# The in-projection's common stage with its pieces moved on every engine, and the recurrence's receptance copied on chip

## The chip, the cores and the metric

The kernel runs on one core of one Trainium2 chip, as a single launch. The metric is the device time of one execution in microseconds; of the kernel before, three runs were timed (2557.12, 2568.69 and 2574.31 us, median 2568.69 us). The engines are called as in the profile: PE is TensorE (PEld its weight loads), DVE is VectorE, ACT is ScalarE, POOL is GpSimd and SP is SyncE, which here only starts DMAs.

## What is computed

Two layers of a flow-matching backbone on 1024 latent and 256 context tokens of width 1024. The even layer has one projection to queries, keys, values, streams of an RWKV-7 mixer and gates; a dense attention and a two-way recurrence read these; an output projection closes the layer. The odd layer has windowed attention in their place. The change lies in the even layer, between its projection and its recurrence. What is computed there, cut from the reference:

```python
p = p + mu * (0.5 * (pp[:, :-2] + pp[:, 2:]) - p)
r, k, v, zw, za = jnp.split(p, ...)
w_log = -jax.nn.softplus(-(w0 + jnp.einsum('btdr,drc->dbtc', jnp.tanh(zw), w2))) - 0.5
decay = jnp.exp(-jnp.exp(w_log))
a = jax.nn.sigmoid(a0 + jnp.einsum('btdr,drc->dbtc', za, a2))
kkf = heads(k * k_k)
kk = kkf / jnp.maximum(jnp.sqrt(jnp.sum(kkf * kkf, axis=-1, keepdims=True)), 1e-12)
kmod = k * (1 + (a - 1) * k_a)
# recurrence, per direction d, head and token, with b = kk * a
S = S * w_t - (S kk_t) b_t + v_t k_t ;   y_t = S r_t
bonus = sum(r * kmod * rk) * v
```

The kernel runs the recurrence in chunks of 64 tokens, so the stage before it has to leave in memory, for each direction, four streams (receptance, removal key, b and key), each multiplied by the exponential of a running sum of decay rates, up or down.

## The kernel before

**Stages.** The program is a sequence of stages on one core: `in0`, the projection of layer 0 (`projected`, from 0 to 672 us of the span), `chunked_scan` (to 1254), dense attention (to 1584), an output projection (to 1765), the projection of layer 1 (to 2095), window attention (to 2446) and the last output projection.

**The order of `in0`.** A hand-written list `order` holds ten steps that turn tokens, then 84 units. A unit is one job's weight block (128 output columns) over one segment of tokens: 28 jobs by three segments, 512, 512 and 256 tokens. It takes 24 matmuls (three split products by eight blocks of the inner dimension, `split_products`, L164). Each engine has its own loop over `order` and its own in-order program; semaphores tie them. At unit i PE computes product i, ACT reads unit i-1 out (at the units of gates with a silu), and DVE finishes unit i-1: for a gate one multiplication of 0.68 us per 512 tokens (L857), at a job's end the split of the weights of the job after next into two parts (L847, L849), and for a mix job the blend with the neighbours (L864, L867). POOL adds the neighbours of a mix job (L700) and issues the stores.

**Jobs.** `jobs0` is: two gates (units 0 to 5), key (6 to 8), value (9 to 11), four queries (12 to 23), fourteen mix jobs (24 to 65), six gates (66 to 83). The first two mix jobs are the low-rank inputs z of the rates; the twelve others are key, receptance and value of four pairs of heads.

**The common stage.** Between the units each engine runs pieces of what makes the streams: `items` has 60 pieces, four pairs of heads by (5 N + 10 X), each on 256 tokens. An N piece normalises a block of keys: a square on ACT, a sum over the head on PE (`squares`, L1132), a clamp on DVE (L938), reciprocal root and square on ACT (L592, L594), and three DVE operations (`unit_keys`, L944 to L950). An X piece makes the streams of one direction: two small matmuls on PE (`loras`, L1142 and L1143), two tanh and a scaling on ACT (`rates`), a scan and a subtraction on DVE (`sums`, L961 and L963), three exponentials on ACT (`exponentials`, L617 to L620), seven DVE multiplications (`products`, L976 to L993), at every second piece two more (`bonus_of`) and the turning of the values on PE and ACT (`turn_values`, L1150, `values_out`, L635), and the stores on POOL.

`slot_of_unit` says which pieces run at which unit, and each engine's `slot(t)` which part of which piece. Before, pieces start at unit 40, the first five at one per unit and then 1.35 per unit; on PE a unit's pieces stand behind its product, and each engine takes the parts of piece t or t-1. SP loads the inputs of the pieces from unit 37 on (`load_z` L437, with `CLEAR_AT` 36: POOL clears buffers that alias those of earlier units first), then keys and receptances as they become ready.

**The recurrence.** `chunked_scan` walks 20 groups in software-pipelined periods. A group has a tile `L` of streams (two directions, two pairs) and a tile `RI`, in which an identity and the receptance lie side by side; `RI` has two buffers. Its identity part is loaded once per buffer (16 DMAs, L1298), its receptance part by eight DMAs per group from the streams in memory (`load_reads`, L1272), though the same values are in `L` already. DVE adds it to a product at `EQ`, which waits for the loads (`r_in`).

## Time and profile before

| | us |
|---|---|
| median of three runs | 2568.69 (2557.12 to 2574.31) |
| profiled execution | 2581.38 |
| its span | 2579.6 |
| PE busy | 2130.2 (83%) |
| DVE busy | 1292.5 (50%) |
| ACT busy | 871.7 (34%) |
| POOL busy | 722.2 (28%) |
| mean granted clock of PE | 0.916 |

The span is the time from the first to the last instruction that the profiler recorded; the execution's own time is 1.8 us more. The profiled execution lies 12.7 us (0.5%) above the median. The busy share of PE is an average over stages with different limits, so the rows further down are of single stages: the units with pieces (313 to 627 us), the end of `in0`, and the recurrence. The clock is a share of full speed (1.0 is 2.4 GHz, 0.5 is 1.2 GHz).

### The profile page before, as it was taken

Reading aid. Unit: us, or ns where it says so; the run is one execution under the profiler, and the core shown is the slowest. Engines: PE = TensorE matmul, PEld = TensorE weight load, DVE = VectorE, ACT = ScalarE, POOL = GpSimd, SP = SyncE. Lnnn points to the kernel's source line nnn. Section 1 sums busy time; section 2 is a strip of 40 time slices with the busy share of each in tenths; the row PEclk is TensorE's granted clock in tenths of the full one; section 3 lists DMA queues with packets and bytes.
Section 4 is the critical chain, followed back from the end, with each engine's and each line's share of the span. In section 5 each row is a group of like instructions: output and inputs, shape, how many; then the busy total and the mean of one; then the engine's idle time right before and its main releaser. Section 6 shows DMA issues by size and latency. Waiting matters only on the chain. (4 is left out here: it accounts for less than half of the span.)

```text
span 2579.6 us, 61157 instructions
## 1 busy us (share of the span) xinstructions
PE 2130.2 (83%) x26174; PEld 1790.7 (69%) x26174; DVE 1292.5 (50%) x2064; ACT 871.7 (34%) x1685; POOL 722.2 (28%) x786
## 2 busy tenths in 40 slices
PE   3899998787367888878599996894999969999988
PEld 1667876565257777777488885673777758888866
DVE  4335467886334444444354443985546524444422
ACT  2223144465234434444133332222334302333311
POOL 2246322211123224233041000343357414100012
PEclk6999998898589999999799997896999979999989
DMA  8556444553322222220321104644344453111162
GB/s 296 180 145 161 131 143 152 180 182 127 112 80 80 64 81 70 61 86 24 87 82 42 42 27 138 189 140 162 105 110 110 112 140 99 58 50 51 39 201 90
DMA packets 228941, 285.70 MB, mean 111 GB/s; under 512 B 61529, under 2 KB 166905, under 8 KB 227649
## 3 DMA queue, kind: packets, MB, share of 16 engines
q1 hardware_dynamic: 190624, 176.52, 22.9%
q0 software_dynamic: 25680, 81.58, 9.9%
q10 hardware_dynamic: 12368, 23.70, 3.1%
q8 instruction: 209, 3.42, 0.6%
q14 instruction: 60, 0.48, 0.1%
HBM read 193.76 MB, written 87.95 MB: 109 GB/s over the span
## 5 line engine op out<-in xcount | busy, mean ns | idle before, releaser
L164 PE MATMUL in_acc<-in_hi,in_whi 128*128 128x512 f32 (+1 forms) x1024 | 400.6, 391 | 19.6 <-DVE in_lo L840 17.6
L164 PE MATMUL in_acc<-in_lo,in_whi 128*128 128x512 f32 (+1 forms) x1024 | 379.6, 371 | 0.0
L164 PE MATMUL in_acc<-in_hi,in_wlo 128*128 128x512 f32 (+1 forms) x1024 | 379.4, 371 | 0.0
L164 PEld LDWEIGHTS in_acc<-in_hi,in_whi 128*128 128x128 f32 x1024 | 199.2, 195 | 72.3 <-issue 42.3
L164 PEld LDWEIGHTS in_acc<-in_lo,in_whi 128*128 128x128 f32 x1024 | 199.2, 195 | 35.2 <-issue 5.3
L164 PEld LDWEIGHTS in_acc<-in_hi,in_wlo 128*128 128x128 f32 x1024 | 198.5, 194 | 33.2
L1939 DVE TENSOR_REDUCE window_top<-window_score 128x1 f32<-128x640 f32 (+1 forms) x128 | 101.3, 791 | 185.2 <-PE window_score L2022 185.1
L1939 DVE TENSOR_REDUCE dense_top<-dense_score 128x1 f32<-128x640 f32 (+1 forms) x144 | 112.3, 780 | 162.0 <-PE dense_score L2026 161.8
L2064 PEld LDWEIGHTS dense_outs<-dense_V,dense_p 128*128 128x128 f32 x1344 | 169.5, 191 | 8.5 <-ACT dense_p L1907 4.9
L2064 PE MATMUL dense_outs<-dense_V,dense_p 128*128 128x65 f32 x1344 | 169.9, 269 | 0.9 <-ACT dense_p L1907 0.8
L2064 PE MATMUL window_outs<-window_V,window_p 128*128 128x65 f32 x1216 | 160.8, 276 | 1.6 <-ACT window_p L1907 1.1
L2064 PEld LDWEIGHTS window_outs<-window_V,window_p 128*128 128x128 f32 x1216 | 153.2, 195 | 9.1 <-ACT window_p L1907 2.6
L1460 DVE TENSOR_TENSOR scan_X<-scan_X,scan_small 128x512 f32<-128x512 f32 x80 | 55.0, 688 | 188.3 <-PE scan_small L1588 187.1
L1593 PE MATMUL scan_wide<-scan_XT,scan_Y 64*64 64x64 f32 x3200 | 120.8, 223 | 24.9 <-issue 24.7
L2238 POOL MEMSET close_eps<- 128x1 f32 x2 | 0.2, 103 | 474.5 <-POOLq L127 474.5
L1338 POOL TENSOR_TENSOR scan_DG<-scan_LB,scan_lmask 128x512 f32<-128x512 f32 x20 | 25.3, 1266 | 382.9 <-ACT scan_LB L1374 382.9
L1907 ACT ACTIVATE dense_p<-dense_turned 128x512 f32<-128x512 f32 x168 | 96.1, 597 | 107.7 <-PE dense_turned L2050 107.2
L164 PE MATMUL close_acc<-w_hi,close_hi 128*128 128x512 f32 x288 | 117.3, 407 | 18.2 <-DVE close_lo L2312 18.2
L1569 PE MATMUL scan_small<-scan_X,scan_off 64*64 64x64 f32 x3200 | 119.9, 226 | 11.2 <-issue 10.4
L1593 PEld LDWEIGHTS scan_wide<-scan_XT,scan_Y 64*64 64x64 f32 x3200 | 106.7, 135 | 25.0 <-issue 24.9
L1347 POOL TENSOR_TENSOR scan_off<-scan_LA,scan_lmask 128x512 f32<-128x512 f32 x100 | 124.0, 1274 | 0.0
L1388 ACT ACTIVATE scan_Y<-scan_small 128x512 f32<-128x512 f32 x100 | 59.7, 597 | 189.8 <-PE scan_small L1569 189.8
(268 smaller groups left out, 5161.6 us busy)
## 6 DMA issues: line engine op xcount, KB each, us to landing
streams<-in_streams_out POOLq DMA_DIRECT2D x40, 512.0 KB, 3.8
scan_L<-streams SPq DMA_DIRECT2D x80, 256.0 KB, 3.7
in_wl<-in_w_mod ACTq DMA_DIRECT2D x32, 512.0 KB, 4.5
in_raw<-in_w_in_even SPq DMA_DIRECT2D x28, 512.0 KB, 4.3
in_raw<-in_w_in_odd SPq DMA_DIRECT2D x20, 512.0 KB, 4.0
close_ga<-gates SPq DMA_DIRECT2D x18, 512.0 KB, 4.1
in_wm<-in_w_mod SPq DMA_DIRECT2D x8, 1024.0 KB, 12.3
gates<-in_outs POOLq DMA_DIRECT2D x32, 256.0 KB, 3.7
```

The lines of the kernel that those rows point to most:

```text
L164: last = pe.matmul(out, a(k), b(k), start=(k == 0 and x == 0), stop=(k == n - 1 and x == 2))
L1338: pool.tensor_tensor(DG[:], LB[:], lmask[:, 0:1, :].to_broadcast([P, NU, HD]), ALU.mult).then_inc(diagonal, 1)
L1347: pool.tensor_tensor(off[s][:, k], triangles, lmask[:, k + 1:k + 2, :].to_broadcast([P, NU, HD]), ALU.mult).then_inc(off_done, 1)
L1388: act.activation(Y[s][:], small[s][:], ACT.Copy).then_inc(y_read[s], 1)
L1460: dve.tensor_tensor(X[s][:], X[s][:], small[s][:], ALU.subtract).then_inc(x_less[s], 1)
L1569: return pe.matmul(small[s][half_of(1 - c), u, :], off[s][half_of(c), k, u, :], X[s][half_of(c), u, :], start=True, stop=True)
L1593: return pe.matmul(wide[s][half_of(1 - c), u, :], Y[s][half_of(1 - c), u, :], XT[j % 3][half_of(1 - c), u, :], start=True, stop=True)
L1907: act.activation(p[:, s % NP_], turned[s % NTURN][:], ACT.Exp, scale=SCALE).then_inc(expd, 1)
L1939: dve.tensor_reduce(top[:, i % NSLOT, x, r:r + 1], score[:, :, 0:width], AXS, ALU.max).then_inc(topped, 1)
L2064: last = pe.matmul(outs[i % 2][:, r * HW:(r + 1) * HW], p[:, s % NP_, r * P:(r + 1) * P], v, start=(k == 0 and r == 0), stop=(k == n - 1 a ...
L2238: pool.memset(eps[:, 0:1], EPS).then_inc(readied, 1)
```

## The change

It does the following.

1. **Pieces.** They start at unit 38 and are spread evenly, 63 slots (60 pieces and three to flush) over 50 units. A slot t issues parts of different pieces: on PE the first low-rank product of piece t+2, the second of t+1, the squares of t+1 and the turned values of t-1, and all of it stands ahead of the unit's product; on ACT the exponentials of t-1, rates of t+1, roots of t-1, squares of t+2, values out of t-2; on DVE first the last part (unit keys, products, bonus) of t-2 and then clamp or sums of t; on POOL the stores of t-3.
2. **One exponential less.** A tile `falls` holds the falling exponential with one extra column of ones per chunk, so that the receptance reads it at one offset and the removal key at the other; DVE's subtraction and ACT's second exponential are gone, and a POOL memset is added. DVE's scaling of `km` moves to ACT. `sigs` and `km` get more buffers. The squares go to a PSUM bank of their own (`aux` 3), the second low-rank product has one bank in place of two.
3. **Loads of z.** Two DMAs in place of four.
4. **Jobs.** Five mix jobs come first (units 0 to 14), then key, value, queries (15 to 32), nine mix jobs (33 to 59) and all eight gates (60 to 83).
5. **Recurrence.** `load_reads` is gone; ACT copies the receptance from `L` into `RI` (four copies of 64x256 per group). `RI` has three buffers, so 24 identity loads in place of 16, and SP's load of the streams of group a+2 waits for the copies of group a too.

```diff
-    CLEAR_AT, N_AT = 36, 40
+    CLEAR_AT, N_AT, FLUSH = 36, 38, 3
-        slot_of_unit[u] = min(len(items) + 1, max(0, min(u - N_AT, NSG) + max(0, (u - N_AT - NSG) * 27 // 20)))
+        slot_of_unit[u] = max(0, u - N_AT) * (len(items) + FLUSH) // (NU + 4 - N_AT)
...
 # SP, load_z
-                    sp.wait_ge(cleared, 3)
+                    sp.wait_ge(cleared, 4)
                     sp.dma_start(tz[:], rkvz[12]).then_inc(z_in, 16)
-                    for d in range(2):
-                        sp.dma_start(za[(1 - d) * HD:(2 - d) * HD], rkvz[13][d * HD:(d + 1) * HD]).then_inc(z_in, 16)
-                        sp.dma_start(a2s[(1 - d) * HD:(2 - d) * HD], a2[d]).then_inc(dc_in, 16)
+                    sp.dma_start(za[:], rkvz[13]).then_inc(z_in, 16)
+                    sp.dma_start(a2s[:], a2.rearrange("d r n -> (d r) n")).then_inc(dc_in, 16)
...
 # ACT, rates(b, s, d)
+                    act.wait_ge(sig_done, n + 1)
+                    if q >= 2:
+                        act.wait_ge(bon_sum, q - 1)
+                    act.activation(km[:, q % 2, d], sigs[:, n % 3], ACT.Identity, scale=kac[:, b:b + 1], bias=kan[:, b:b + 1]).then_inc(mixed_k, 1)
 # ACT, exponentials(b, s, d)
-                    act.activation(e_to[:], cum[:, h], ACT.Exp, scale=-DECAY).then_inc(exp_to, 1)
-                    act.activation(before[:, h], before[:, h], ACT.Exp, scale=-DECAY).then_inc(exp_in, 1)
+                    act.activation(falls[:, d, :, 1 - d:CHUNK + 1 - d], cum[:, h].rearrange("p (c n) -> p c n", n=CHUNK), ACT.Exp,
+                                   scale=-DECAY).then_inc(exp_to, 1)
 # ACT, slot(t)
                     if item(t - 1)[0] == "X":
                         exponentials(*item(t - 1)[1:])
...
+                    if item(t + 1)[0] == "X":
+                        rates(*item(t + 1)[1:])
+                    if item(t - 1)[0] == "N":
+                        root_keys(*item(t - 1)[1:])
+                    if item(t + 2)[0] == "N":
+                        square_keys(*item(t + 2)[1:])
+                    if item(t - 2)[0] == "X" and item(t - 2)[3] == 1:
+                        values_out(*item(t - 2)[1:3])
...
 # DVE, slot(t)
+                    if item(t - 2)[0] == "N":
+                        unit_keys(*item(t - 2)[1:])
+                    if item(t - 2)[0] == "X":
+                        products(*item(t - 2)[1:])
+                        if item(t - 2)[3] == 1:
+                            bonus_of(*item(t - 2)[1:3])
                     if item(t)[0] == "N":
                         clamp(*item(t)[1:])
                     if item(t)[0] == "X":
                         sums(*item(t)[1:])
-                    if item(t - 1)[0] == "N":
-                        unit_keys(*item(t - 1)[1:])
-                    if item(t - 1)[0] == "X":
-                        products(*item(t - 1)[1:])
-                        if item(t - 1)[3] == 1:
-                            bonus_of(*item(t - 1)[1:3])
...
 # PE
                 def squares(b, s):
                     q = q_of(b, s)
-                    side_free()
+                    if q >= 1:
+                        pe.wait_ge(clamped, q)
                     pe.wait_ge(squared_k, q + 1)
-                    pe.matmul(side[:, 0:SG], block1[:], ksq[:, q % 2], start=True, stop=True).then_inc(squares_in, 1)
+                    pe.matmul(aux[:, 3, 0:SG], block1[:], ksq[:, q % 2], start=True, stop=True).then_inc(squares_in, 1)
+                def lora_of_a(b, s, d):
+                    n, half = n_of(b, s, d), slice(d * HD, (d + 1) * HD)
+                    if n >= 1:
+                        pe.wait_ge(sig_done, n)
+                    pe.matmul(aux[:, 2, 0:SG], a2s[half, b * P:(b + 1) * P], za[half, s * SG:(s + 1) * SG], start=True, stop=True
+                              ).then_inc(lora_a, 1)
                 def slot(t):
                     if t == 0:
                         pe.wait_ge(tanhed, 1)
-                    if item(t)[0] == "N":
-                        squares(*item(t)[1:])
-                    if item(t)[0] == "X":
-                        loras(*item(t)[1:])
-                        if item(t)[3] == 1:
-                            turn_values(*item(t)[1:3])
+                        squares(0, 0)
+                    if item(t + 2)[0] == "X":
+                        lora_of_w(*item(t + 2)[1:])
+                    if item(t + 1)[0] == "X":
+                        lora_of_a(*item(t + 1)[1:])
+                    if item(t + 1)[0] == "N":
+                        squares(*item(t + 1)[1:])
+                    if item(t - 1)[0] == "X" and item(t - 1)[3] == 1:
+                        turn_values(*item(t - 1)[1:3])
...
                     else:
+                        for t in slots(what, i):
+                            slot(t)
                         if i < NU:
                             product(i)
...
-                    for t in slots(what, i):
-                        slot(t)
...
 # recurrence
-        RI = [st.sb(f"RI{s}", [P, NU, P]) for s in range(2)]
+        RI = [st.sb(f"RI{s}", [P, NU, P]) for s in range(3)]
...
                         sp.wait_ge(gram_in, 2 * a + 2)
+                        sp.wait_ge(reads_done, a + 1)
                         load_streams(a + 2)
...
-                    if c is not None and c + 2 < NG:
-                        sp.wait_ge(eq_read, 2 * c + 2)
-                        load_reads(c + 2)
...
+                def reads(j):
+                    s = j % 2
+                    act.wait_ge(l_in[s], uses(j) * 4 * 16)
+                    if j >= 3:
+                        act.wait_ge(eq_read, 2 * (j - 3) + 2)
+                    for c in range(2):
+                        for h in range(2):
+                            last = act.activation(RI[j % 3][half_of(c), 4 * h:4 * h + 4, half_of(c)].rearrange("p (d g) n -> p d g n", g=2),
+                                                  L[s][half_of(h), :, :, half_of(c)], ACT.Copy)
+                    last.then_inc(reads_done, 1)
...
                     if a is not None:
                         turned_out(a, 2)
+                        reads(a)
...
-    jobs0 = (gates[:2] + key_jobs(QC, AKV, kst0) + value_jobs(QC + AKV * HD, AKV, v0) + query_jobs(0, AH, qst0, 3) + mixes
-             + gates[2:])
+    jobs0 = (mixes[:5] + key_jobs(QC, AKV, kst0) + value_jobs(QC + AKV * HD, AKV, v0) + query_jobs(0, AH, qst0, 3) + mixes[5:]
+             + gate_jobs(GA, gates0, 3))
```

How the order of instructions moves is shown at two places.

**VectorE, in a gate's unit with a weight split, where the last X piece of a pair of heads meets the first N pieces of the next.** `in_whi` and `in_wlo` are the two parts of the split weights, `in_norm` the clamped sum of squares, `in_outs` the gated output of the unit. Before:

```order
L857 SCALAR_TENSOR_TENSOR in_outs<-in_xs,in_acc 128x256 [waits in0_out_stored2,in0_sig]
L847 CAST in_whi<-in_raw 128x1024 [waits in0_summed,in0_w_in0]
L849 TENSOR_TENSOR in_wlo<-in_raw,in_whi 128x1024 [waits in0_w_high]
L938 TENSOR_SCALAR in_norm<-in_side 128x256 [waits in0_unit,in0_squares_in]
L976 SCALAR_TENSOR_TENSOR in_b_<-in_sigs,in_kk 128x256 [waits in0_b_done,in0_kd_done,in0_unit,in0_sig_done]
L979 TENSOR_SCALAR in_km<-in_sigs,in_kac,in_kan 128x256
L982 TENSOR_TENSOR in_km<-in_km,in_rkv 128x256 [waits in0_rkv_in0,in0_mixed_k]
L986 TENSOR_TENSOR in_streams_out<-in_rkv,in_e_to 128x2x128 [waits in0_exp_to,in0_s_stored1]
L988 TENSOR_TENSOR in_streams_out<-in_kk,in_before 128x2x128 [waits in0_exp_in]
L991 SCALAR_TENSOR_TENSOR in_streams_out<-in_b_,in_cum 128x2x128 [waits in0_b_made,in0_exp_from]
L993 TENSOR_TENSOR in_streams_out<-in_km,in_cum 128x2x128 [waits in0_km_done]
L999 TENSOR_TENSOR in_bon<-in_km 128x256 [waits in0_bon_stored]
```

With the change, at the same place of the pieces (the end of a pair's X pieces):

```order
L863 SCALAR_TENSOR_TENSOR in_outs<-in_xs,in_acc 128x256 [waits in0_out_stored2,in0_sig]
L853 CAST in_whi<-in_raw 128x1024 [waits in0_summed,in0_w_in0]
L855 TENSOR_TENSOR in_wlo<-in_raw,in_whi 128x1024 [waits in0_w_high]
L987 SCALAR_TENSOR_TENSOR in_b_<-in_sigs,in_kk 128x256 [waits in0_b_done,in0_unit,in0_sig_done]
L990 TENSOR_TENSOR in_km<-in_km,in_rkv 128x256 [waits in0_rkv_in1,in0_mixed_k]
L994 TENSOR_TENSOR in_streams_out<-in_rkv,in_falls 128x2x128 [waits in0_exp_to,in0_s_stored1]
L995 TENSOR_TENSOR in_streams_out<-in_kk,in_falls 128x2x128
L998 SCALAR_TENSOR_TENSOR in_streams_out<-in_b_,in_cum 128x2x128 [waits in0_b_made,in0_exp_from]
L1000 TENSOR_TENSOR in_streams_out<-in_km,in_cum 128x2x128 [waits in0_km_done]
L1006 TENSOR_TENSOR in_bon<-in_km 128x256 [waits in0_bon_stored]
L1008 SCALAR_TENSOR_TENSOR in_bon<-in_rkv,in_rkc,in_bon 128x256 [waits in0_bon_sum]
L944 TENSOR_SCALAR in_norm<-in_aux 128x256 [waits in0_unit,in0_squares_in]
```

The clamp (`in_norm`, from `in_aux` now and from `in_side` before) stands behind the last part of the X piece, where it stood ahead of it; the subtraction and the scaling of `km` are no longer in the row of operations.

**TensorE, at a unit that takes two X pieces.** `in_aux` takes the low-rank products, `in_side` the turned values, `in_acc` the unit's product. Before:

```order
L1142 MATMUL in_aux<-in_tz,in_w2s 128x256 [waits in0_sig_done,in0_rate_t]
L1143 MATMUL in_aux<-in_za,in_a2s 128x256
L1142 MATMUL in_aux<-in_tz,in_w2s 128x256 [waits in0_sig_done,in0_rate_t]
L1143 MATMUL in_aux<-in_za,in_a2s 128x256
L1150 MATMUL in_side<-in_ident,in_rkv 128x128 [waits in0_rkv_in1,in0_values_read,in0_clamped]
L1150 MATMUL in_side<-in_ident,in_rkv 128x128
L164 MATMUL in_acc<-in_hi,in_whi 128x256 [waits in0_gated,in0_low,in0_w_low]
```

With the change:

```order
L164 MATMUL in_acc<-in_hi,in_wlo 128x512
L1140 MATMUL in_aux<-in_tz,in_w2s 128x256 [waits in0_rate_t]
L1147 MATMUL in_aux<-in_za,in_a2s 128x256 [waits in0_sig_done]
L1156 MATMUL in_side<-in_ident,in_rkv 128x128 [waits in0_rkv_in0,in0_values_read]
L1156 MATMUL in_side<-in_ident,in_rkv 128x128
L1140 MATMUL in_aux<-in_tz,in_w2s 128x256 [waits in0_rate_t]
L1147 MATMUL in_aux<-in_za,in_a2s 128x256 [waits in0_sig_done]
L164 MATMUL in_acc<-in_hi,in_whi 128x256 [waits in0_gated,in0_low,in0_w_low]
```

The last row of each is the first matmul of a 256 wide product: before that of the next unit, now that of the pieces' own unit. Before, the six matmuls stood behind their unit's product; now they stand ahead of their own unit's product, and each second low-rank product (L1147) waits for ACT to have read the one before (`in0_sig_done`), where before two banks took turns.

## Rows read from the trace of the kernel before

**Rows 1.** Windows: us; PE, PEld, DVE, ACT, POOL busy (count); clock; DMA share; GB/s.
```profile
313.00:627.00 314.00, 268.75 (x1329) 213.61 (x1329) 239.11 (x485) 156.39 (x381) 73.94 (x94) 0.91 0.49 157
627.00:672.00 45.00, 4.97 (x20) 2.06 (x18) 25.86 (x67) 14.93 (x44) 7.50 (x14) 0.56 0.40 135
760.00:1254.00 494.00, 394.43 (x15475) 369.68 (x15467) 230.99 (x383) 202.04 (x374) 148.44 (x120) 0.97 0.22 63
```

**Rows 2.** Waits of TensorE from 313 to 627 us: total us, times, longest us.
```profile
PE in_side L1132 <- issue: 20.4, 3, 9.3
PE in_side L1150 <- ACT in_vt_out L635: 13.7, 4, 4.6
```

**Rows 3.** Timeline of TensorE: first matmuls of three products (512, 256 and 512 wide).
```profile
308.00 0.39 PE L164 MATMUL in_acc<-in_hi,in_whi 128*128 128x512 f32 x1
...
313.44 0.28 PE L164 MATMUL in_acc<-in_hi,in_whi 128*128 128x256 f32 x1
...
316.31 0.40 PE L164 MATMUL in_acc<-in_hi,in_whi 128*128 128x512 f32 x1
```

**Rows 4.** Timeline of VectorE over one X piece: start us, us, what, [idle before, releaser].
```profile
619.23 0.69 DVE L961 TENSOR_TENSOR_SCAN in_cum<-in_carry,in_rate 128x256 f32<-128x256 f32 x1
619.95 0.42 DVE L963 TENSOR_TENSOR in_before<-in_cum,in_rate 128x256 f32<-128x256 f32 x1
...
622.75 0.68 DVE L857 SCALAR_TENSOR_TENSOR in_outs<-in_xs,in_acc 128x512 f32<-128x512 f32 x1
624.86 0.69 DVE L961 TENSOR_TENSOR_SCAN in_cum<-in_carry,in_rate 128x256 f32<-128x256 f32 x1 [1.42 <-ACT in_rate L604]
```

**Rows 5.** Timeline of ScalarE: an X piece from its first exponential, and a table load.
```profile
562.34 0.42 ACT L617 ACTIVATE in_e_to<-in_cum 128x256 f32<-128x256 f32 x1 [2.58 <-issue]
...
565.51 0.58 ACT L523 ACTIVATE in_xs<-in_acc 128x512 f32<-128x512 f32 x1
...
590.96 1.28 ACT L523 ACT_TABLE_LOAD   x1
592.25 0.60 ACT L523 ACTIVATE in_xs<-in_acc 128x512 f32<-128x512 f32 x1
```

**Rows 6.** Timeline around the start of the pieces: VectorE, SyncE's queue twice, TensorE.
```profile
303.53 3.23 DVE L849 TENSOR_TENSOR in_wlo<-in_raw,in_whi 128x1024 fp32r<-128x1024 f32 x1
...
307.28 0.50 SPq L439 DMA_DIRECT2D in_tz<-rkvz  x1
...
319.45 0.50 SPq L455 DMA_DIRECT2D in_k_all<-rkvz  x1
...
327.22 0.59 PE L1132 MATMUL in_side<-in_ksq,in_block 128*128 128x256 f32 x2
```

**Rows 7.** Timeline of VectorE over an N piece behind a weight split.
```profile
599.54 0.69 DVE L847 CAST in_whi<-in_raw 128x1024 fp32r<-128x1024 f32 x1
...
601.40 0.42 DVE L938 TENSOR_SCALAR in_norm<-in_side 128x256 f32<-128x256 f32 x1
...
602.65 0.48 DVE L950 SCALAR_TENSOR_TENSOR in_kk<-in_k_all,in_kkn,in_norm 128x256 f32<-128x256 f32 x1
```

**Rows 8.** Timeline: VectorE's last operation of the first stage.
```profile
657.61 0.48 DVE L1001 SCALAR_TENSOR_TENSOR in_bon<-in_rkv,in_rkc,in_bon 128x256 f32<-128x256 f32 x1
```

**Rows 9.** Timeline at the start of the recurrence: SyncE's queue three times, TensorE.
```profile
680.19 10.40 SPq L1298 DMA_DIRECT2D scan_RI<-in_consts  x16
690.64 5.57 SPq L1272 DMA_DIRECT2D scan_RI<-streams  x8
...
720.10 5.15 SPq L1272 DMA_DIRECT2D scan_RI<-streams  x8
...
731.77 1.97 PE L1531 MATMUL scan_gram<-scan_ident,scan_L 128*128 128x128 f32 x8 [18.79 <-DMA scan_L<-streams]
```

**Rows 10.** Timeline of ScalarE in the middle of the recurrence.
```profile
980.06 0.77 ACT L1402 ACTIVATE scan_YO<-scan_sums 64x256 f32<-64x256 f32 x2 [0.78 <-PE scan_sums L1690]
985.03 0.60 ACT L1388 ACTIVATE scan_Y<-scan_small 128x512 f32<-128x512 f32 x1 [4.21 <-PE scan_small L1569]
```

More of the change, by code:

```diff
@@ L232, in slots @@
             return range(0)
-        return range(slot_of_unit[i], len(items) + 1 if i == NU + 3 else slot_of_unit[i + 1])
+        return range(slot_of_unit[i], slot_of_unit[i + 1])
     def item(t):
@@ L334, in projected @@
             k_all, kk = st.sb("k_all", [P, TOK]), st.sb("kk", [P, TOK])
-            ksq, root, norm = (st.sb(n, [P, 2, SG]) for n in ("ksq", "root", "norm"))
+            ksq, root, khalf, norm = (st.sb(n, [P, 2, SG]) for n in ("ksq", "root", "khalf", "norm"))
             rkv = st.sb("rkv", [P, 2, 3, SG])
-            rate, sigs, cum, before = (st.sb(n, [P, 2, SG]) for n in ("rate", "sigs", "cum", "before"))
-            e_to, b_, bon = (st.sb(n, [P, SG]) for n in ("e_to", "b_", "bon"))
-            km = st.sb("km", [P, 2, SG])
+            rate, cum = (st.sb(n, [P, 2, SG]) for n in ("rate", "cum"))
+            sigs = st.sb("sigs", [P, 3, SG])
+            falls = st.sb("falls", [P, 2, SG // CHUNK, CHUNK + 1])
+            b_, bon = (st.sb(n, [P, SG]) for n in ("b_", "bon"))
+            km = st.sb("km", [P, 2, 2, SG])
             streams_out = st.sb("streams_out", [P, 2, PT, 4 * P])
@@ L475, in _ @@
                     for b in range(PAIRS):
-                        done = unit_of(items.index(("N", b - 1, NSG - 1)) + 1) + 1 if b else 0
+                        done = unit_of(items.index(("N", b - 1, NSG - 1)) + 2) + 1 if b else 0
                         loads.append((max(CLEAR_AT + 1, ready(2 + 3 * b), done), 2, load_keys, (b,)))
@@ L760, in clear @@
                     pool.memset(carry[:, 1, CHUNK - 1::CHUNK], 0.0).then_inc(cleared, 1)
+                    pool.memset(falls[:], 1.0).then_inc(cleared, 1)
                     pool.memset(halves[:], 0.5).then_inc(prepared, 1)
@@ L1265, in load_values @@
                                      ).then_inc(v_in[s], 16)
-                def load_reads(j):
-                    s, r = j % 2, j % 2
-                    for d in range(2):
-                        for g in range(2):
-                            for c in range(2):
-                                sp.dma_start(
-                                    RI[s][half_of(c), unit(0, d, g):NU:4, half_of(c)],
-                                    streams[d, 2 * r + g, :, tile(j, d), c * CHUNK:(c + 1) * CHUNK].rearrange(
-                                        "(h k) n -> k h n", h=2)).then_inc(r_in[s], 16)
                 def store(j):
@@ L1292, in _ @@
                 load_values(1)
-                for s in range(2):
+                for s in range(3):
                     for c in range(2):
```

119 lines of the change are left out of this document (48 added, 71 removed).

## The prediction

> **What bounds the kernel now.** I read the windows by stage first. From 313 to 627 us, the units of the first stage that carry pieces, TensorE is busy 268.75 of 314 us, VectorE 239.11 and ScalarE 156.39 [rows 1]: TensorE sets the pace there, VectorE is close behind, and TensorE's 45.3 us of idle time are what a new order can win in this stretch. The waits say where they lie: 20.4 us ahead of the squares, three times, 9.3 us at most, and 13.7 us ahead of the turned values, for ScalarE to empty the shared bank [rows 2]. A product of 512 tokens takes 5.44 us at full clock (308.00 to 313.44), one of 256 takes 2.87 us [rows 3], so three units take 13.78 us, if the first two are alike. Behind the last product, from 627 to 672 us, TensorE does 4.97 us of work and VectorE 25.86 [rows 1]: the pieces that are left are the path. In the recurrence TensorE is busy 394 of 494 us [rows 1].
>
> The sum is made against the profiled execution, 2581.38 us (span 2579.6 and 1.8 around it). It lies 12.7 us above the median of 2568.69; I carry the difference over to the median.
>
> **Term 1, idle time removed.** The new banks and the later parts take away both waits of [rows 2] and the small ones: -45.3. TensorE also loses clock after idle time: the granted clock is 0.91 there [rows 1]. Fifteen rounds of three units and a 256 at full clock are 15 x 13.78 + 2.87 = 209.6 us; some 46 us are the pieces' matmuls (an estimate: 40 X at 1.0 and 20 N at 0.4, less those of the tail, fits it); 268.75 - 209.6 - 46 leaves 13. That is 0.29 us for each us idle. Removed: -58.3.
>
> **Term 2, waits added on TensorE.** Its pieces now stand ahead of their unit's product, so whatever a piece waits for holds the product and all later ones.
> - Start. SyncE loads the pieces' inputs in 12.7 us, from 307.28 to 319.45 + 0.5; the first squares come 7.8 us after the last of them was issued [rows 6]. Now the pieces start at unit 38, and two loads of about 0.9 us are gone. Unit 36 starts at T, 302.56 by [rows 3]; the loads started at T + 4.7. Query stores now run until just before, and POOL clears only when they have landed: T + 6.5 (estimate; 4.7 is the lower end, 8.5 the upper). Last load issued at T + 6.5 + 10.4, squares at T + 24.7; unit 38 is due at T + 10.9. Stall 14 us.
> - Squares. Each waits for the clamp of the piece before, which VectorE does in the same unit, behind the unit's gate, a split if there is one, and now behind the last part of another piece (the rows of VectorE's order above). From the end of TensorE's previous product: the read 0.60 [rows 5], gate 0.68 [rows 4], clamp 0.42 [rows 7], products 2.1. The last is the X piece's 3.52 us (619.23 to 622.75) less the scan, 0.72, the subtraction, 0.42, and the scaling, about 0.3 [rows 4]. So 3.8 us with nothing else; 5.7 with the split of 1.86 (599.54 to 601.40) [rows 7]; 5.9 with the bonus (0.48 [rows 8] and about as much again) and a table load of 1.28 [rows 5]. Together 15.4 per pair, and two pairs have their N pieces in gate units: 30.8. In the mix units there is one stall of 4.3 (a split that POOL's neighbour sums slow, 0.69 [rows 7] + 3.23 [rows 6], and the clamp) and one of 7.0 (with read and products too). Together 42.
> - Two X pieces in one unit, five times. The second low-rank product waits until ScalarE has done its read (0.60), the exponentials and the rates; [rows 5] give 3.17 us from the first exponential to the end of the rates, with one exponential more. I take 2.8 less TensorE's own 0.5: 2.3 each, 11.5.
> - Clock: 0.29 x (14 + 42) = 16; the short waits I leave out.
>
> Together +84. Net with term 1: **+25**. Bounds: if none of the squares' waits shows, -42 and their 12 of clock; if the clock stays at its lower level through the N phases, see the second rival.
>
> **Term 3, the end of the stage.** The last product ends by 627, where TensorE's work all but stops [rows 1], and VectorE ends at 657.61 + 0.48 = 658.1 [rows 8]: 31.1 us, because the X piece takes 5.2 us in the tail: VectorE waits 1.42 us for the rates [rows 4] and as much for the exponentials. With the new order the parts are a slot apart, so VectorE runs through: five products 10.5, three bonuses 2.6, three scans 2.2, the last gate 0.9, that is 16.2. **-15**. Lower end -19 (fewer pieces left), upper -5 (ScalarE still late, as in [rows 5], 3.17 us per piece and now one more operation).
>
> **Term 4, ScalarE's tables.** The built program has 41 table loads in place of 32: three fewer while the tokens are turned, twelve more among the pieces, where silu's and the exponential's tables now alternate. A load takes 1.28 us, and the next operation starts 1.29 us after it began [rows 5]. ScalarE has 157 us idle in the stretch [rows 1], so the twelve (15 us) cost only where TensorE waits, which is in term 2; of the three gone I count one, **-1.3**. The Trainium skill ("ScalarE: Activation LUTs", section "What ACT_TABLE_LOAD costs") gives 1283 ns and 1380 ns more for a drain, 2.66 us for each switch. The load agrees with the row; the drain is not seen there, since the following read starts at once. By the page twelve loads would be 32 us, still under ScalarE's idle time, and the sum would be 2.8 us higher, for the two on which TensorE waits.
>
> **Term 5, the recurrence.** At its start SyncE issues sixteen identity loads in 10.40 us and two sets of eight receptance loads, 5.57 and 5.15 us, and TensorE waits 18.79 us for streams queued behind them [rows 9]. Now 24 identity loads, +5.2, and no receptance loads, -10.7: **-5.5**. Later groups: ScalarE's four copies of 64x256 are some 1.3 us per group (estimate: two such copies out of PSUM take 0.77 [rows 10], so 1.5 at most). ScalarE is busy 202 of 494 us [rows 1], and its waits are for TensorE, 4.21 and 0.78 us [rows 10]; both hold or nearly hold the copy: 0. Bounds: +10, if 0.5 us per group stays uncovered (1.3 less 0.78, 20 groups), and -20, third rival. DVE's subtraction, POOL's memset and the moved stores lie beside TensorE's work: 0; a third buffer and later stores need no wait that a row shows.
>
> **Sum:** +25.6 - 14.9 - 1.3 - 5.5 = +3.9: 2585 against the profiled 2581.38, **2573 us** against the median.
>
> **Rivals.**
> 1. *Faster: the clamps are not late.* If VectorE runs ahead of TensorE, or the squares of most N pieces share a unit in which TensorE waits anyway, only the start (14), the double units (11.5), some 20 of the squares and 5 of clock stay, 50 in place of 84. 2573 - 34 = 2539 us. For it: VectorE has 75 us idle in the stretch [rows 1], and its work falls by 0.7 us per X piece. Against: the wait is one of order within a unit, not of load.
> 2. *Slower: the clock does not come back in the N phases.* Each unit of the four N phases holds TensorE 4 to 6 us, about as long as its product runs. A 512 wide product at half clock is 5.44 us longer [rows 3]. The sum has three such products in 16 us; if five more run so, +27: 2600 us. It decides from about four more. For it: before, the clock mean was 0.91 with only seven long waits. Against: the tail of an N phase has waits of 3.8 us, in which the weight loads go on.
> 3. *The recurrence gets faster.* 160 loads of 32 KB in rows of 256 B go away. If part of its TensorE idle time (100 us [rows 1]) was theirs, -20: 2553 us. Against: the DMA share is 0.22 there [rows 1], and no wait in the middle of the stage names them. The Trainium skill ("DMA: Bandwidth & Descriptors", section "Specifications") asks for 512 B at least per transfer for line rate, which speaks for this rival.
> 4. *The change's gain in the pieces isn't had:* turned values wait again, since values_out is behind the exponentials now; +5, inside the range.
>
> **Chances.** Forecast 0.44, rival 1 0.29, rival 2 0.20, rival 3 0.07. A measurement of this kernel tells 1% from no change, that is 2543 to 2594. Faster by over 1%: rival 1 nearly whole and the lower edge of the forecast, 0.31. Slower: most of rival 2 and the forecast's upper edge (start at 8.5, copies uncovered at +10), 0.22. Same: 0.47. The range: 2573 less 34 and a few us for term 3's lower end and part of rival 3, 2532; above, rival 2, 2600. Some 0.2 stays outside.
>
> **What would show it.** TensorE's waits at the squares should name VectorE's clamp (L944), some eight of 4 to 7 us, and one of about 14 us near unit 38; at L1147 five of 2 us that name ScalarE's tanh. The waits at L1132 and L1150 of before should be gone. From the last product to VectorE's last operation of the stage: 16 us. Table loads between gates' reads and exponentials, 1.28 us each. TensorE's first wait for the recurrence's streams: 13 us in place of 18.79; ScalarE's copies in the recurrence without a TensorE wait behind them. I am wrong in term 2 if the sum of TensorE's waits in the piece units is under 35 us, in term 3 if VectorE still waits in the tail, and in term 5 if the recurrence changes by more than 10 us.

## The result, and the profile after

The change is slower: 2607.37 us median of four runs (2597.22 to 2608.30) against 2570.48 us (2557.12 to 2574.31), a ratio of 1.0143 with an interval of 1.0112 to 1.0174, or some 37 us. The forecast was 2573 us, with a range up to 2600. The profiled execution took 2606.56 us (span 2604.8), 25.2 us more than the profiled one of before. (One execution of before and three of the kernels further down ran in a slower state; they are left out of the medians.)

The windows of the change, by the same stages as [rows 1] (the pieces' units now end at 689, the first stage at 718; columns as there):

```profile
313.00:689.00 376.00, 299.43 (x1340) 230.14 (x1339) 217.07 (x433) 193.74 (x414) 67.46 (x99) 0.86 0.41 133
689.00:718.00 29.00, 2.85 (x10) 1.08 (x6) 14.86 (x41) 8.37 (x24) 5.19 (x10) 0.53 0.43 155
802.00:1276.00 474.00, 388.68 (x15325) 365.37 (x15321) 229.96 (x381) 226.67 (x434) 147.84 (x119) 0.97 0.18 57
```

The units with pieces grew from 314 to 376 us, though VectorE's work fell from 239 to 217 us; the granted clock went from 0.91 to 0.86. The end of the stage shrank from 45 to 29 us. The table splits each trace at the same events: the end of product 37, the end of the last product, the first DMAs of the recurrence and of the dense attention. "Waits" are TensorE's gaps over 0.3 us. "Slow products" is what the 46 products took beyond 5.23 us (2.75 us for 256 tokens), from the start of the first matmul to the start of the last. "Other" is the remainder: products at full clock, and the pieces' own matmuls at whatever clock.

| us | before | change | difference |
|---|---|---|---|
| up to product 37 | 313.2 | 313.1 | -0.1 |
| units with pieces | 313.6 | 375.6 | +62.0 |
| - waits | 45.1 | 76.2 | +31.1 |
| - slow products | 18.2 | 33.0 | +14.8 |
| - other | 250.4 | 266.4 | +16.0 |
| last product to recurrence | 45.5 | 29.1 | -16.4 |
| recurrence | 584.0 | 558.0 | -26.0 |
| all behind it | 1323.2 | 1329.0 | +5.8 |

The sum is +25.3. The last row is code that the change does not touch.

TensorE's waits from 313 to 690 us (engine, output and line, what ended the wait; total us, times, longest), where [rows 2] had the squares behind "issue" and the turned values:

```profile
PE in_aux L1134 <- DVE in_norm L944: 42.2, 10, 7.3
PE in_aux L1134 <- ACT in_ksq L585: 17.0, 3, 7.0
PE in_aux L1147 <- ACT in_sigs L608: 8.6, 5, 3.1
PE in_side L1156 <- ACT in_vt_out L639: 4.6, 5, 1.2
PE in_aux L1140 <- ACT in_rate L602: 4.2, 4, 1.1
```

The longest wait for a clamp, in the timelines of VectorE and TensorE:

```profile
419.00 0.69 DVE L853 CAST in_whi<-in_raw 128x1024 fp32r<-128x1024 f32 x1 [3.94 <-PE in_acc L164]
419.73 3.22 DVE L855 TENSOR_TENSOR in_wlo<-in_raw,in_whi 128x1024 fp32r<-128x1024 f32 x1
422.87 0.41 DVE L987 SCALAR_TENSOR_TENSOR in_b_<-in_sigs,in_kk 128x256 f32<-128x256 f32 x1
...
425.73 0.42 DVE L944 TENSOR_SCALAR in_norm<-in_aux 128x256 f32<-128x256 f32 x1
```

```profile
426.21 1.22 PE L1134 MATMUL in_aux<-in_ksq,in_block 128*128 128x256 f32 x2 [7.32 <-DVE in_norm L944]
426.87 0.99 PE L164 MATMUL in_acc<-in_hi,in_whi 128*128 128x512 f32 x1
427.66 0.63 PE L164 MATMUL in_acc<-in_lo,in_whi 128*128 128x512 f32 x1
...
431.07 0.63 PE L164 MATMUL in_acc<-in_hi,in_whi 128*128 128x512 f32 x1
431.50 0.45 PE L164 MATMUL in_acc<-in_lo,in_whi 128*128 128x512 f32 x1
431.78 0.39 PE L164 MATMUL in_acc<-in_hi,in_wlo 128*128 128x512 f32 x1
```

VectorE starts the split only when the previous product has ended (419.00); it takes 3.9 us, the last part of an X piece 2.9 us (from 422.87), and then comes the clamp (425.73). TensorE stands for 7.32 us with the next product ready behind the squares. When it goes on, the matmuls come 0.43 us apart (the 1.2 GHz level) until 431.5, and 0.23 us apart, as at 2.4 GHz, only then.

VectorE's end of the stage and ScalarE's tables, answering to [rows 8, 5]:

```profile
703.73 0.48 DVE L1008 SCALAR_TENSOR_TENSOR in_bon<-in_rkv,in_rkc,in_bon 128x256 f32<-128x256 f32 x1
```

```profile
533.84 1.28 ACT L524 ACT_TABLE_LOAD   x1 [11.64 <-PE in_acc L164]
535.14 0.60 ACT L524 ACTIVATE in_xs<-in_acc 128x512 f32<-128x512 f32 x1
535.75 1.28 ACT L592 ACT_TABLE_LOAD   x1
537.04 0.42 ACT L592 ACTIVATE in_root<-in_norm 128x256 f32<-128x256 f32 x1
```

VectorE ends 15.6 us behind the last product (688.6 to 704.2), where it took 31.1. The next operation starts 1.29 to 1.30 us after a table load began, twice more.

ScalarE in the recurrence, with the copies; they answer to [rows 10]:

```profile
980.59 1.69 ACT L1368 ACTIVATE scan_RI<-scan_L 64x256 f32<-64x256 f32 x4
982.30 0.77 ACT L1405 ACTIVATE scan_YO<-scan_sums 64x256 f32<-64x256 f32 x2
985.71 0.60 ACT L1391 ACTIVATE scan_Y<-scan_small 128x512 f32<-128x512 f32 x1 [2.64 <-PE scan_small L1573]
```

The four copies take 1.69 us, and ScalarE still waits for TensorE behind them. Its busy time in this stretch rose from 202 to 227 us with none of it at TensorE.

### The profile page after: what moved, and what is told of

It reads as the page before. It is cut to its first block and busy times, and to the rows that moved or that the text cites. A ratio compares the mean times of both kernels' runs of the same rounds, so it can differ in the third digit from the quotient of the medians.

```text
span 2604.8 us, 60988 instructions
## 1 busy us (share of the span) xinstructions
PE 2162.6 (83%) x26174; PEld 1810.9 (70%) x26174; DVE 1256.4 (48%) x1984; ACT 932.3 (36%) x1774; POOL 719.5 (28%) x787
## 3 DMA queue, kind: packets, MB, share of 16 engines
q1 hardware_dynamic: 168704, 171.52, 21.5%
## 5 line engine op out<-in xcount | busy, mean ns | idle before, releaser
L164 PE MATMUL in_acc<-in_hi,in_whi 128*128 128x512 f32 (+1 forms) x1024 | 409.1, 399 | 21.5 <-DVE in_lo L846 19.0
L164 PE MATMUL in_acc<-in_lo,in_whi 128*128 128x512 f32 (+1 forms) x1024 | 386.0, 377 | 0.0
L164 PE MATMUL in_acc<-in_hi,in_wlo 128*128 128x512 f32 (+1 forms) x1024 | 384.9, 376 | 0.0
L164 PE MATMUL close_acc<-w_hi,close_hi 128*128 128x512 f32 x288 | 117.4, 408 | 18.2 <-DVE close_lo L2316 18.2
L1330 POOL TENSOR_TENSOR scan_DG<-scan_LB,scan_lmask 128x512 f32<-128x512 f32 x20 | 25.3, 1265 | 357.8 <-ACT scan_LB L1377 357.8
L1573 PEld LDWEIGHTS scan_small<-scan_X,scan_off 64*64 64x64 f32 x3200 | 107.1, 139 | 13.3 <-issue 12.1
```

What stands on the lines that cost most here:

```text
L164: last = pe.matmul(out, a(k), b(k), start=(k == 0 and x == 0), stop=(k == n - 1 and x == 2))
L1330: pool.tensor_tensor(DG[:], LB[:], lmask[:, 0:1, :].to_broadcast([P, NU, HD]), ALU.mult).then_inc(diagonal, 1)
L1573: return pe.matmul(small[s][half_of(1 - c), u, :], off[s][half_of(c), k, u, :], X[s][half_of(c), u, :], start=True, stop=True)
```

## The experiments

Ten kernels ran, in three sessions; the median of before was 2575 to 2576 us in each. The change itself was not timed in them; its ratio of 1.0143 makes it 2613 us there, and the times below are set against that. The ratio's interval is some 8 us to either side, so a distance from the change of 12 us or less is hardly clear of noise in the times. The split of the units is finer: each kernel was cut at the same events as above, and kernels with the same first stage agree within 2.4 us in it (375.6 and 373.2 for the change and `dead loads`, 313.6 and 313.4 for before and `recurrence alone`). It is one trace of each:

| us | waits | slow products | other | units with pieces | to recurrence | recurrence | median |
|---|---|---|---|---|---|---|---|
| recurrence alone | 43.7 | 19.3 | 250.5 | 313.4 | 45.5 | 569.0 | 2567.6 |
| all pieces behind | 16.9 | 15.1 | 256.4 | 288.5 | 31.6 | 567.3 | 2529.2 |
| squares behind | 33.8 | 16.9 | 258.2 | 308.8 | 29.1 | 567.9 | 2543.0 |
| two banks | 43.9 | 21.9 | 260.1 | 325.9 | 29.1 | 563.9 | 2565.8 |
| clamp first | 63.2 | 24.7 | 264.5 | 352.3 | 29.1 | 570.3 | 2601.0 |
| filled waits | 35.2 | 21.5 | 305.2 | 361.9 | 29.1 | 565.0 | 2601.9 |
| old jobs | 73.9 | 31.3 | 265.6 | 370.8 | 29.7 | 567.2 | 2617.1 |
| dead loads | 76.2 | 31.1 | 265.9 | 373.2 | 29.1 | 581.4 | 2628.6 |
| behind, two banks | 9.9 | 8.3 | 254.7 | 272.8 | 31.6 | 571.7 | 2514.0 |
| the same, unit 40 | 18.6 | 10.9 | 260.2 | 289.6 | 31.6 | 564.6 | 2532.6 |

**TensorE's pieces behind the product.** The theory is that their place ahead of it makes the loss; the rival, that VectorE and ScalarE are too slow for the new slots.

```diff
-                        for t in slots(what, i):
-                            slot(t)
                         if i < NU:
                             product(i)
...
+                    for t in slots(what, i):
+                        slot(t)
```

> The change with one thing put back: on TensorE the pieces of a unit stand behind its product again. Theory (TensorE's order makes the loss): VectorE's clamp and ScalarE's tanh are done while the product runs, so most of the 76 us of waits at the pieces and most of the clock lost behind them go: the first stage 60 to 75 us shorter, about 2540 us. Rival (VectorE and ScalarE cannot keep up with the pieces in that order, and their lateness only shows at TensorE): the waits move to the product, less than 25 us are gained, 2582 us or more.

It ran 2529.18 us, ratio 0.9823 (0.9794 to 0.9852) to before, 84 us under the change. Waits fell from 76.2 to 16.9 us, the units from 375.6 to 288.5, by 87 us where the theory had 60 to 75. The rival falls: with the same work on the other engines, nothing waits in their place.

```profile
309.00:598.00 289.00, 271.14 (x1335) 213.57 (x1333) 213.76 (x427) 191.65 (x410) 68.41 (x97) 0.95 0.53 172
```

VectorE's 214 and ScalarE's 192 us are those of the change, in 289 us in place of 376: the engines had the room. The clock is 0.95.

**The squares alone behind.**

```diff
-                    if item(t + 1)[0] == "N":
-                        squares(*item(t + 1)[1:])
...
                             product(i)
...
+                    for t in slots(what, i):
+                        if item(t + 1)[0] == "N":
+                            squares(*item(t + 1)[1:])
```

> The change with the squares alone behind their unit's product; low-rank products and turned values stay ahead of it. Theory (the squares' waits are the loss, the low-rank products' waits of 17 us are the smaller part): from the start of unit 38 to the last product about 305 us in place of 376, between the 288 of all pieces behind and the 326 of two banks; 2613 - 70 = 2543 us. Rival (what helped was to take the low-rank products from in front of the product, since the rates then wait for nothing): 340 us or more there, 2575 us.

2542.98 us, ratio 0.9893 (0.9849 to 0.9937), as the theory had it: 308.8 us for the units. So 67 of the 87 us between the change and all pieces behind are the squares'; the other 20 come with the low-rank products and turned values.

**Two banks for the squares.** The bank of the second low-rank product is idle in an N phase. (Halves of one bank would be simpler. The Trainium skill, "PSUM — Partial Sum Buffer", section "PSUM bank collisions raise a hardware error", says that two engines in the same bank and the same 32 partitions at once raise an error; the squares fill all 128 partitions. No run here shows it.)

```diff
 # DVE, clamp
-                    dve.tensor_scalar(norm[:, q % 2], aux[:, 3, 0:SG], ...
+                    dve.tensor_scalar(norm[:, q % 2], aux[:, 3 - s % 2, 0:SG], ...
...
 # PE, squares
                     if q >= 1:
-                        pe.wait_ge(clamped, q)
+                        pe.wait_ge(clamped, q if s == 0 else q - 1)
+                    if s % 2 and b:
+                        pe.wait_ge(sig_done, n_of(b, 0, 0))
                     pe.wait_ge(squared_k, q + 1)
-                    pe.matmul(aux[:, 3, 0:SG], block1[:], ksq[:, q % 2], ...
+                    pe.matmul(aux[:, 3 - s % 2, 0:SG], block1[:], ksq[:, q % 2], ...
...
 # lora_of_a
+                    if s == 0 and d == 0:
+                        pe.wait_ge(clamped, q_of(b, 3) + 1)
```

> The change with the squares taking turns between two PSUM banks (the odd blocks of a pair in the bank of the second low-rank product, which is idle then), so that a sum of squares waits for the clamp before the last. TensorE's pieces stay ahead of the product. Theory: six waits go (4.5, 7.3, 6.0, 4.6, 6.0, 4.6 us, 33 in all) and with them some 13 us of lowered clock: about 2561 us. Rival (VectorE is behind by as much): the 33 us show again as waits of the products or of the next piece, under 12 us gained, 2595 us or more.

2565.78 us: 47 us under the change where 46 were expected, with TensorE's order untouched. TensorE's waits from 309 to 637 us:

```profile
PE in_aux L1136 <- ACT in_ksq L585: 24.5, 5, 7.3
...
PE in_aux L1136 <- DVE in_norm L944: 2.0, 3, 1.4
```

The clamp waits fell from 42.2 to 2.0 us. Part of them shows again behind ScalarE's square of the keys, 24.5 where it was 17.0: that square is the last thing that ScalarE does in such a slot.

**The clamp ahead of the products on VectorE.**

```diff
                     if item(t - 2)[0] == "N":
                         unit_keys(*item(t - 2)[1:])
+                    if item(t)[0] == "N":
+                        clamp(*item(t)[1:])
                     if item(t - 2)[0] == "X":
                         products(*item(t - 2)[1:])
...
-                    if item(t)[0] == "N":
-                        clamp(*item(t)[1:])
```

> The change with VectorE's clamp ahead of the last part of the X piece in its slot, TensorE's order as in the change. Theory (a part of each clamp wait is the products of 2.1 us in front of it): about eight waits get 2.1 us shorter, 17 us, and 6 of clock: 2613 - 23 = 2590 us. Rival (the wait is for the unit's gate and the weight split, the products lie beside it): under 8 us gained, 2605 us or more.

2600.99 us, 12 us under the change: between the two, and hardly clear of noise. The waits for clamps fell by 13.5 us (42.2 to 28.7), as

```profile
PE in_aux L1134 <- DVE in_norm L944: 28.7, 9, 4.6
```

shows, and slow products by 8.3; the pieces' units are 23 us shorter in the trace, the theory's size, while the medians moved half as much (the profiled execution, 2587.44 us, is the fastest of its four). So the products are a third of the clamp's lateness. That the gate, the split and the read behind the ended product are the rest is read from the timeline above and was not tested by itself.

**The waits filled with matmuls.**

```diff
+                    for k in range({2: 8, 5: 8, 7: 14, 10: 11, 11: 7, 12: 12, 13: 9, 16: 7, 17: 12, 18: 9}.get(q, 0)):
...
+                        pe.matmul(acc[u % NA][:, 0:SG], w2s[0:HD, 0:P], tz[0:HD, 0:SG], start=True, stop=True)
                     if q >= 1:
                         pe.wait_ge(clamped, q)
```

> The change with matmuls of no use in front of the squares that wait for a clamp, into the bank that the unit's product overwrites, 97 of 64x128x256, about as long as each wait. They remove no wait. Theory (the lost clock is a cost of its own, about 28 us beside 76 us of waiting): the products behind the filled waits run at full clock, 12 to 25 us gained, 2582 to 2595 us. Rival (the products are slow there for another reason, or the clock would have fallen anyway): no gain, and up to 8 us more where the filling is longer than the wait, 2607 to 2615 us.

2601.86 us, 11 us under the change. The intervals of the two ratios overlap (1.0077 to 1.0156 against 1.0112 to 1.0174), so by the times this is the weak edge of the theory or nothing; the trace is clearer. In it 41 of the 76 us of waits are matmuls now, slow products fell from 33.0 to 21.5 us, and the units from 375.6 to 361.9.

```profile
310.00:672.00 362.00, 326.36 (x1532) 254.23 (x1532) 216.98 (x433) 193.62 (x414) 67.45 (x99) 0.93 0.42 138
```

The clock is 0.93 for 0.86. The filling lets no result come sooner, so these 14 us are the price of the lowered clock behind the filled waits, and it comes on top of the waits.

**The old order of the jobs.**

```diff
-    jobs0 = (mixes[:5] + key_jobs(...) + value_jobs(...) + query_jobs(...) + mixes[5:] + gate_jobs(GA, gates0, 3))
+    gates = gate_jobs(GA, gates0, 3)
+    jobs0 = (gates[:2] + key_jobs(...) + value_jobs(...) + query_jobs(...) + mixes + gates[2:])
```

> The change with the jobs in the order of before (two gates, key, value, queries, fourteen mixes, six gates). Theory (the loss is in the pieces' order on TensorE, not in the jobs'): the waits at the squares are there again, ten or so of 4 to 7 us, and the time is within 12 us of the change, 2601 to 2625 us. Rival (the gates' silu tables and stores beside the pieces make the loss): 25 us or more faster, 2588 us or less.

2617.05 us, ratio 1.0176 (1.0120 to 1.0232), 4 us from the change, and 370.8 us for the units: the jobs' order is not the cause.

**The recurrence alone** (the kernel before with the change's `chunked_scan`).

> The kernel before with the recurrence of the change alone (receptance copied by ScalarE, three buffers). In the trace of the change the recurrence took 558 us in place of 584: 7 us less up to its first output, and its 20 groups came every 26.1 us in place of 27.1. Theory: the recurrence gains by itself, so 2570 - 26 = 2544 us, with the first stage as before. Rival: it gains only because it starts later, when the stores of the stage before have drained; then about 2563 us, the 7 us of the start alone.

2567.6 us, ratio 0.9964 (0.9941 to 0.9986): 9 us (4 to 15), near the rival's figure and not the 26 of the trace. The recurrence took 569.0 us in its trace; in the nine other traces with the loads gone, the change's own included, it took 558.0 to 571.7. The profiled execution of the change had the shortest, so the 26 us of the table overstate what the copies give. That the traces differ by 25 us and the medians by 37 has another reason: the profiled execution of before lies 10.9 us above its median, that of the change 0.8 below. In all ten the first output is read 83.7 to 86.9 us after the start (90.5 before), and from there to the end they take 474 to 486 us against 493. The before side of this is a single trace.

**The loads put back, unread** (`load_dead` is the `load_reads` of before with tiles that nobody reads as its target).

```diff
+                load_dead(0)
+                load_dead(1)
...
+                    if c is not None and c + 2 < NG:
+                        sp.wait_ge(eq_read, 2 * c + 2)
+                        load_dead(c + 2)
```

> The change with the receptance loads of before put back into the recurrence, into two tiles that nobody reads (same queue, same sizes, same place); the copies of ScalarE stay the ones that are used. Theory (the loads themselves slow the recurrence, by their rows of 256 B or their place in SyncE's queue): the recurrence takes 575 to 590 us again in place of 558 to 569, 2613 + 20 = 2633 us. Rival (VectorE's wait for these loads made it slow): it stays at 558 to 569 but for some 10 us at the start, about 2620 us.

2628.59 us, 16 over the change, ratio 1.0204 (1.0170 to 1.0238): between the two, with the recurrence of the theory, 581.4 us. Against the change's trace 10 us are the start (first output at 94.3), and 487.0 from there to the end. At the start the loads cost their issue time on SyncE:

```profile
735.33 11.85 SPq L1280 DMA_DIRECT2D scan_dead<-streams  x16
```

Whether the loads also slow the groups (487.0 against 474 to 486) a single trace of each cannot tell; it stays open.

**Both mends, and a later start.** `behind_two_banks` has the edits of the first and the third experiment; its sister starts the pieces at unit 40.

```diff
-    CLEAR_AT, N_AT, FLUSH = 36, 38, 3
+    CLEAR_AT, N_AT, FLUSH = 36, 40, 3
```

> Both mends together: pieces behind their product on TensorE, and two banks for the squares. Theory (what is left with the pieces behind is 8.8 us of clamp waits and the start): 8 us of waits and some 4 of clock less than with the pieces behind alone, 276 us from unit 38 to the last product in place of 288.5, about 0.5% faster than that kernel, 2518 us. Rival (the ends of VectorE's and ScalarE's work set the pace by now): no more than 3 us gained, 2526 to 2530 us.

> The same with the pieces starting at unit 40 in place of 38 (63 slots over 48 units). Theory (the first squares wait 4.4 us for their inputs from memory, which are there two units later): these 4.4 us and some 3 of clock go, but more units carry two pieces, which costs 1 to 3 us: 2513 to 2517 us. Rival (more units with two pieces cost as much as the start gives): as the kernel with unit 38, or slower.

The first ran 2514.01 us, ratio 0.9724 (0.9673 to 0.9775) to before: 61 us faster than before by the medians, 71 by the ratio, and some 99 faster than the change, with all its other parts kept. The theory had 2518 us and 276 us for the units; they took 272.8. From 311 to 584 us:

```profile
311.00:584.00 273.00, 262.17 (x1333) 206.72 (x1333) 213.31 (x426) 191.80 (x408) 68.58 (x97) 0.99 0.56 182
```

The clock is 0.99, and TensorE is busy 96% of the stretch. The later start lost: 2532.6 us, 19 us more. The 4.4 us of waiting for the inputs went, but 63 slots over 48 units put two pieces in more units, and other waits of 13 us came: TensorE waits for the rates and the turned values of ScalarE, and for squares and clamps. From 311 to 600 us:

```profile
PE in_aux L1142 <- ACT in_rate L602: 6.7, 4, 2.8
PE in_aux L1136 <- ACT in_ksq L585: 4.2, 2, 3.9
PE in_aux L1136 <- DVE in_norm L944: 3.8, 3, 1.7
PE in_side L1160 <- ACT in_vt_out L639: 3.7, 5, 2.0
```

The units took 16.8 us more, where the expectation had 4 to 6 us less; its 1 to 3 us for the fuller units were the part that was too low.

## Why the prediction was wrong

**Term 2, the waits added on TensorE, is the step that failed: the waits' cause was right, the size of the term too small, above all the clock that they cost.** Net of term 1 it was to be +25 and is +62.0. The two parts of the difference:

- *The waits themselves*, 67.5 us forecast, 76.2 measured. The start: 14 forecast, 7.6 measured (7.0 for the first squares, 0.6 for the second). Clamps: 42 forecast, 41.6 measured (42.2 less that 0.6). Units with two X pieces: 11.5 forecast, 17.4 measured (8.6 + 4.6 + 4.2). Missed altogether were 10 us, the other two waits behind `in_ksq`, where the first squares of a pair share a unit with an X piece and wait for ScalarE's square of the keys, its last operation there. That makes +9. That it is no more is part luck: the start was put 6.4 us too high, which hides as much of the 16 that were missed. SyncE began the loads 4.2 us after T, not 6.5, and the squares started at 320.46, T + 17.9 in place of T + 24.7.
- *The clock*, 16 us forecast for the added waits against 13 for the removed, 3 us net; measured 15 us more in slow products and 16 more in the pieces' own matmuls and what lies between. So 28 us of the 37 that were missing lie here, at most 24 of them the clock's. Two of the 16 are matmuls that came from the stage's end (TensorE's work there fell from 4.97 to 2.85 us), and `behind_two_banks`, at a clock of 0.99, still has 254.7 us in "other", 4.3 more than before; that leaves at most 12. I priced lowered clock by the microsecond of waiting (0.29) and left the short waits out. For before that price was right: seven products there are over 0.5 us slow, 13.4 us in all. In the change they are 16, 29.3 us in all; each costs 1.8 us on average, where it was 1.9, behind 1.0 to 7.7 us of waiting in its unit. So the cost goes more by the number of such units than by the length of the waits. The pieces' own matmuls slow down too: the squares behind the 7.32 us wait took 1.22 us, two without a wait 0.59 in [rows 6]. The filled waits show that this is a cost by itself.

The cause under both was forecast and is shown: all pieces behind the product removes 87 us, the squares alone 67, a second bank 50, each without lightening another engine.

**Term 3**, the end of the stage: -14.9 forecast, -16.4 measured; VectorE's run of 16.2 us took 15.6. (Two slips of the working, 13.78 for 13.75 us per three units and 5.9 for 6.0 us at a bonus, move the sum by less than 1 us.)

**Term 4**, the tables: nothing shows of the 1.3 us ahead of the pieces (-0.1). The drain that the Trainium skill ("ScalarE: Activation LUTs", section "What ACT_TABLE_LOAD costs") adds to a switch is not in this trace either: 1.29 us from load to next operation.

**Term 5**, the recurrence: -5.5 at the start forecast, -6.8 measured to the first output. Its copies cost nothing that shows, as forecast, though they take 1.69 us for 1.3: no engine but SyncE's queue, before it loads the next streams, waits for them in the trace. The prediction called this term wrong if the recurrence changed by more than 10 us; by the traces it did (12 to 26 us), by the times of the recurrence alone (9 us) it did not. The third rival's gain in the groups is there in part, 7 to 19 us by the traces, 9 us for the whole stage change by the medians.

**The rivals.** The second, slower one named the right side and not the mechanism. It took whole products at half clock, 5.44 us more for each, and needed about four more of them. No product of 512 tokens was that slow: in each the matmuls of 128x512 were 0.23 us apart again after at most 5.7 us, and the dearest lost 2.7 us. What came was nine more products 1.8 us slow, 16 us in all, as much as three of its. Its argument against was a wrong reading: the weight loads do not go on in the waits (ahead of the squares at 513.54 us they had stood for 4.26 us, beside a wait of 3.84). The first was out: the clamps' waits are 41.6 us, where it left some 20. The fourth rival's turned values wait 4.6 us as it said. VectorE's and ScalarE's load never bound, which `behind_two_banks` shows.

**What was wrong in weighing.** The terms came out at +3.9 with the largest ones of opposite sign (-58 and +84), each uncertain by ten or twenty. The chance of a slower kernel should have been the largest: the added waits were derived one by one from rows, and every omission of such a list (the other waits in units with two pieces, the ScalarE square, short waits) makes it longer.

## What to carry to other kernels

Small work of another chain that is put ahead of the bounding engine's long work must have all its inputs ready when its turn comes; behind the long work most of the same waiting is covered (76.2 us of waits became 16.9 here). Count a wait on TensorE twice: its length, and what the lowered clock behind it costs. Here that was 0.9 to 2.7 us for each slow product, 1.8 on average, behind waits from 1 us on, though some waits below 2 us cost nothing. And where a wait is for a buffer's last reader, look for a bank that is idle in that phase before reordering engines: here it took 50 us out of the units with a small edit.

## What the runs showed of the hardware

- Behind a wait of 7.32 us the product's matmuls of 128x512 came 0.43 us apart for 4.6 us and then 0.23; behind one of 2.10 us, in the kernel with all pieces behind the product, they started 0.43 apart as well, and that product lost 1.7 us (TensorE's timeline there):

```profile
394.13 0.70 PE L1134 MATMUL in_aux<-in_ksq,in_block 128*128 128x256 f32 x2 [2.10 <-DVE in_norm L944]
394.81 0.74 PE L164 MATMUL in_acc<-in_hi,in_whi 128*128 128x512 f32 x1
395.35 0.63 PE L164 MATMUL in_acc<-in_lo,in_whi 128*128 128x512 f32 x1
395.77 0.63 PE L164 MATMUL in_acc<-in_hi,in_wlo 128*128 128x512 f32 x1
```

- Matmuls of no use in the waits lifted the granted clock from 0.86 to 0.93 and gained 14 us in the trace: there, keeping TensorE at work was worth a third of a microsecond for each microsecond filled.
- A wait of the same length is not always followed by the lower clock. Ahead of the same product (unit 62), its matmuls of 128x256 came 0.12 us apart behind 1.79 us in `behind_two_banks`, and 0.21 us apart behind 1.75 us in the kernel with all pieces behind:

```profile
458.90 0.67 PE L1136 MATMUL in_aux<-in_ksq,in_block 128*128 128x256 f32 x2 [1.79 <-ACT in_ksq L585]
...
459.52 0.28 PE L164 MATMUL in_acc<-in_lo,in_whi 128*128 128x256 f32 x1
459.64 0.28 PE L164 MATMUL in_acc<-in_hi,in_wlo 128*128 128x256 f32 x1
```

```profile
462.69 0.78 PE L1134 MATMUL in_aux<-in_ksq,in_block 128*128 128x256 f32 x2 [1.75 <-ACT in_ksq L585]
...
463.49 0.41 PE L164 MATMUL in_acc<-in_lo,in_whi 128*128 128x256 f32 x1
463.70 0.41 PE L164 MATMUL in_acc<-in_hi,in_wlo 128*128 128x256 f32 x1
```

  In the kernel before, waits of 1.64 and 1.95 us cost their product 0.1 us at most. What decides it, the runs do not show.
- The same recurrence code took 558 to 572 us over ten traces: a gain of 10 us in a stage of this length can't be read from one trace of each kernel.
